# A product-key expert mixer: the dense gate array built by GpSimd's accumulating scatters instead of one-hot matmuls

## The reference, cut to what matters

```python
v1, i1 = lax.top_k(s1, PEER_TOPK)          # 16 of 128 rows
v2, i2 = lax.top_k(s2, PEER_TOPK)          # 16 of 128 columns
sc, pos = lax.top_k(comb, PEER_TOPK)       # 16 of their sums
experts = e1 * N_KEYS + e2
gate = jax.nn.softmax(sc, axis=-1)
ue = u[experts]
act = jax.nn.gelu(jnp.einsum('thkd,td->thk', ue, xt)) * gate
return jnp.einsum('thk,thkd->td', act, v[experts])
```

## Time and profile before

| | |
|---|---|
| median of 3 runs | 4715.58 us (4709.3 to 4719.58) |
| the profiled execution | 4713.71 us, of which its span is 4712.1 us |
| busy share of the span | PE 91%, PEld 78%, DVE 72%, ACT 37%, POOL 19% |
| mean granted clock of TensorE | 0.964 of full speed |
| moved by DMA | 913.53 MB, of 487554 packets 228722 under 512 B |
| stage of heads and bridge | 2004 to about 2545 us |
| gate stage | about 2545 to 3240 us |
| tail | about 3240 to 3624 us |
| mix and end | 3624 to 4712 us |

### The profile page before, as it was taken

The page is one execution under the profiler, slowest core; times in us unless marked ns, Lnnn a source line. Parts: engine busy times, 40 slices in busy tenths (PEclk is TensorE's granted clock), DMA queues, the critical chain, the costliest instruction groups (busy, mean ns, idle before and its releaser), DMA issues.

```text
span 4712.1 us, 67213 instructions
## 1 busy us (share of the span) xinstructions
PE 4302.6 (91%) x23716; PEld 3667.5 (78%) x23716; DVE 3409.5 (72%) x6418; ACT 1727.1 (37%) x3205; POOL 916.3 (19%) x885
## 2 busy tenths in 40 slices
PE   6999999999899799899999888888778999999998
PEld 3668877777788587798999777778778788888886
DVE  6530057777477543489997999997566998888888
ACT  3221146556566432322224555554111222222222
POOL 0000000000244210000001333333554222222221
PEclk9999999999999899999999999999899999999999
DMA  6642123332666553322223555556889999999996
GB/s 250 236 171 94 48 86 134 128 122 91 195 189 189 192 185 101 108 88 83 80 91 114 208 208 206 206 206 254 298 315 317 312 303 299 289 289 289 289 289 203
DMA packets 487554, 913.53 MB, mean 194 GB/s; under 512 B 228722, under 2 KB 277250, under 8 KB 482548
## 3 DMA queue, kind: packets, MB, share of 16 engines
q1 hardware_dynamic: 385684, 534.58, 34.7%
q0 software_dynamic: 95840, 363.13, 21.8%
q10 hardware_dynamic: 5760, 12.59, 0.7%
HBM read 722.20 MB, written 187.97 MB: 193 GB/s over the span
## 4 chain that ended last, share of the span: by engine, by line
PE 25%; DVE 24%; DMA 6%; issue 2%; POOL 1%; ACT 0%; SPq 0%; DVEq 0%; ACTq 0%
PE ph_gate_ps L2440 14%; PE ph_hid_ps L2440 7%; DVE held_tiles L2751 5%; DMA ph_ring<-in_u_rows,held_tiles 5%; DVE ph_row_hot L2744 5%; DVE ph_ring L2737 3%; DVE held_tiles L2747 2%; PE ph_hid_ps L2365 2%; PE ph_hid_ps L2355 2%; POOL ph_ring L2323 1%; DVE ph_hot L2627 1%; DVE ph_hot L2634 1%; DVE ph_u_lo L2572 1%; DVE ph_score L2599 1%; DVE ph_index L2601 1%
## 5 line engine op out<-in xcount | busy, mean ns | idle before, releaser
L2365 PE MATMUL ph_hid_ps<-ph_n_hi,ph_u_hi 128*128 128x384 f32 x2048 | 720.9, 352 | 89.6 <-DVE ph_u_lo L2572 89.6
L2365 PE MATMUL ph_hid_ps<-ph_n_lo,ph_u_hi 128*128 128x384 f32 x2048 | 709.0, 346 | 0.0
L2365 PE MATMUL ph_hid_ps<-ph_n_hi,ph_u_lo 128*128 128x384 f32 x2048 | 708.0, 346 | 0.0
L2365 PEld LDWEIGHTS ph_hid_ps<-ph_n_hi,ph_u_hi 128*128 128x128 f32 x2048 | 405.2, 198 | 99.4 <-DVE ph_u_lo L2572 99.2
L2323 POOL DMA_INDIRECT ph_ring<-in_u_rows,held_tiles x256 | 319.4, 1248 | 777.0 <-DVEq L2660 578.0
L2737 DVE CUSTOM_DVE_ANT_0 ph_ring<-ph_ring,ph_n_rows 128x1024 f32<-128x1024 f32 x256 | 308.0, 1221 | 148.2 <-DMA ph_ring<-in_u_rows,held_tiles 147.4
L2365 PEld LDWEIGHTS ph_hid_ps<-ph_n_lo,ph_u_hi 128*128 128x128 f32 x2048 | 404.7, 198 | 0.2
L2365 PEld LDWEIGHTS ph_hid_ps<-ph_n_hi,ph_u_lo 128*128 128x128 f32 x2048 | 403.0, 197 | 0.0
L2341 POOL DMA_INDIRECT ph_ring<-in_v_experts,ph_pick_again x256 | 242.6, 948 | 765.9 <-DVE held_tiles L2837 734.1
L2522 ACT ACTIVATE held_tiles<-held_tiles 128x128 bf16<-128x128 bf16 x768 | 246.1, 390 | 281.6 <-DVE held_tiles L2747 277.3
L2837 DVE SCALAR_TENSOR_TENSOR held_tiles<-ph_ring,ph_factor,held_tiles 128x1024 f32<-128x1024 f32 x254 | 324.5, 1278 | 0.0
(11 more groups left out here) (395 smaller groups left out, 10339.5 us busy)
## 6 DMA issues: line engine op xcount, KB each, us to landing
ph_u_raw<-in_tiles SPq DMA_DIRECT2D x136, 512.0 KB
ph_v_raw<-in_v_experts SPq DMA_DIRECT2D x124, 512.0 KB
scratch_hidden<-ph_hidden SPq DMA_DIRECT2D x128, 384.0 KB
scratch_gate_tiles<-ph_gates SPq DMA_DIRECT2D x12, 4096.0 KB
ph_u_raw<-scratch_hidden SPq DMA_DIRECT2D x124, 384.0 KB
ph_hidden<-scratch_gate_tiles SPq DMA_DIRECT2D x124, 384.0 KB
proj_w_ch<-in_w_ch SPq DMA_DIRECT2D x49, 512.0 KB, 3.8
mb_w_raw<-in_w_branch POOLq DMA_DIRECT2D x48, 512.0 KB, 3.9
```

The source lines that it names most:

```text
L2365: mm = pe.matmul(hid_halves[r][:, c, :], u[r][a][:, k, :], n2[b][:, k, c * CUT:(c + 1) * CUT], start=(k == 0 and a + b == 0), stop=(k == K ...
```

## The change

Gates are no longer computed on PE. A flat array of experts by tokens in memory (16384 x 768 floats, 50 MB) is cleared early in the kernel by 24 DMAs of 2 MB from ACT's queue, spread over the three turns of `project_token_major` (10, 10 and 4). For this the loop over turns is written out. When a head is done, POOL issues 96 indirect DMAs for it (6 token tiles x 16 picks). Each has 128 elements of 4 bytes, one per partition, and adds the weight to the array at expert * 768 + token. Before a head's DMAs, POOL waits until those of the head before it have landed. In heads 4 to 7 two gathers of u rows follow each three scatters. There is no gate stage: behind the bridge there are 80 tiles of the tail's kind, with 3 dot products each from the third on, the rest behind the last. `low` is always DVE's. The loads of the first four blocks of the mix wait for all scatters and for the last hidden stores. Gates are read from memory in rows of 3 KB, where they were pieces of 256 B.

```diff
-                with act.Fori(0, TURNS - 1) as i:
+                def clear(n):
+                    part = d["gates_flat"].rearrange("(c p n) a -> c p (n a)", c=ZEROS, p=P)
+                    act.dma_start(part[n], d["zeros"]).then_inc(zeroed, 16)
...
+                        if n < CLEARS[i]:
+                            clear(sum(CLEARS[:i]) + n)
+                CLEARS = (10, 10, 4)
+                for i in range(TURNS - 1):
...
                 turn(TURNS - 1, OUTS[1][2], True)
+                act.wait_ge(zeroed, 16 * ZEROS)
...
-TAIL_TILE0 = GATE_TILE0 + SM // 16
+TAIL_TILE0 = 1 + PH * PERIOD + BRIDGE
...
+    SCATTERS = MT * TOPK
...
-                    sync.dma_start(to[2][r].rearrange("p (b n) -> p b n", n=GATE_TOK), d["gate_tiles"][:, :, bass.ds(e, 1), :].rearrange(
-                        "b p a n -> p b (a n)")).then_inc(gate_in[r], 16)
+                    sync.dma_start(to[2][r], gate_rows[:, bass.ds(e, 1), :].rearrange("p a n -> p (a n)")).then_inc(gate_in[r], 16)
...
+                for h in range(PH):
+                    sync.wait_ge(scattered[h], 16 * SCATTERS)
+                for j in range(NJ):
+                    load_expert(j, j % 2, 1 if j >= 2 else None, staged_first)
...
-                pool.wait_ge(head_done, PH)
-                for n in range(NRING):
-                    gather_first(n)
-                for j in range(SM // PER_STEP):
...
-                    pool.tensor_tensor(u[r][1][:], u_raw[r][:], u[r][0][:].bitcast(F32), ALU.subtract).then_inc(u_lo[r], 1)
+                def scatter(h, n):
+                    t, k = divmod(n, TOPK)
+                    at = t * P + h * TOPK + k
+                    pool.indirect_dma_start(d["gates_flat"], bass.IndirectOffsetOnAxis(place_of[:, at:at + 1], 0), held[:, 2, at:at + 1], None,
+                                            compute_op=ALU.add).then_inc(scattered[h], 16)
...
+                for h in range(PH):
+                    pool.wait_ge(head_done, h + 1)
+                    if h >= 1:
+                        pool.wait_ge(scattered[h - 1], 16 * SCATTERS)
+                    if h == PH // 2:
+                        pool.wait_ge(hid_mm[1], PERIOD // 2 * (PH - 2) + 1)
+                    for n in range(SCATTERS):
+                        scatter(h, n)
+                        if h >= PH // 2 and n % 3 != 2:
+                            gather(next(gathers))
...
-                def step(j):
-                    tile(j % 2, (GATE_TILE0 + j) // 2)
-                    for b in range(NBANK):
...
-                                mm = pe.matmul(gate_ps[b][:, t, :], row_hot[b][:, t, :], term[n][b][:, t, :], start=(n == 0), stop=(n == 2))
...
-                    if y in FIRST_AT:
-                        high_parts(0, 0, FIRST_AT.index(y), staged_first)
                 act.wait_ge(dotted, PICKS)
                 act.activation(pick_dot, pick_dot, ACT.Gelu).then_inc(pick_gelu, 1)
+                for j in range(NJ):
+                    high_parts(0, 0, j, staged_first)
...
                 def experts_of(h, s, own):
-                    own.of(dve.tensor_copy(expert[:], placef[s][:]))
...
-                    own.of(dve.tensor_copy(chosen[:, 1, :, bass.ds(h, 1), :].rearrange("p t a k -> p t (a k)"), expert[:]))
+                    of, to = placef[s], place_of4[:, :, bass.ds(h, 1), :].rearrange("p t a k -> p t (a k)")
+                    own.of(dve.scalar_tensor_tensor(to[:, 0:MT, :], of[:, 0:MT, :], float(SM),
+                                                    token[:, 0:MT].unsqueeze(2).to_broadcast([P, MT, TOPK]), ALU.mult, ALU.add))
+                    own.of(dve.tensor_copy(to[:, MT:TT, :], of[:, MT:TT, :]))
...
-                    dots(3 if y in FIRST_AT else 5 + (y < 14) if y < TAIL - 1 else PICKS)
+                    dots(0 if y < 2 else 3 if y < TAIL - 1 else PICKS)
                 assert done == PICKS
+                for j in range(NJ):
+                    prepare(0, 0, j, staged_first)
```

More of the change, by code:

```diff
@@ L580, in project_token_major @@
         ahead_in = sp.sem("ahead_in")
+        zeroed = sp.sem("zeroed")
+        ZEROS = 24
+        d["gates_flat"] = nc.dram_tensor("scratch_gates_flat", (NK * NK * SM, 1), F32, kind="Internal").ap()
         OUTS = [("z", 2, ACT.Silu), ("v", 1, ACT.Copy)]
@@ L2053, in stage_peer_topk @@
         chosen = held[:, 0:3, :].rearrange("p a (t h k) -> p a t h k", t=TT, h=PH)
-        chosenT = held[:, 3:6, 0:SM]
+        place_of = held[:, 0, :].bitcast(U32)
+        place_of4 = place_of.rearrange("p (t h k) -> p t h k", t=TT, h=PH)
         pick_weight, pick_dot = held[:, 2, SM:S], held[:, 3, SM:S]
-        pick = held[:, 4, SM:S].bitcast(U32)
+        pick = place_of[:, SM:S]
+        token = sp.sb("token", [P, TT])
         keys = held[:, 6:8, :].rearrange("p a (h n) -> p (a h) n", n=2 * NK)
@@ L2084, in stage_peer_topk @@
             score_ps = first.enter_context(nc.psum_tensor("ph_score_ps", [P, TT, 2 * NK], F32))
[L2085 to L2094, removed]
+        bank = [sp.ps(f"bank{b}", [P, HALF]) for b in range(NBANK)]
         weight0, v0 = ([[sp.sb(f"{name}0{j}_{p}", [P, width], F32R)[:] for p in ("hi", "lo")] for j in range(NJ)]
@@ L2108, in stage_peer_topk @@
         staged = (v_raw, raw, gate)
-        staged_first = tuple([held[:, 2 * n + r, 0:SM if n else D] for r in range(2)] for n in range(3))
+        staged_first = ([held[:, r, :] for r in (6, 7)], [held[:, r, 0:SM] for r in (1, 3)], [held[:, r, 0:SM] for r in (4, 5)])
         acc = held
@@ L2119, in stage_peer_topk @@
         rstd = sp.sb("rstd", [P, TT])
-        out_ps = [gate_ps[b][:].rearrange("p t n -> p (t n)") for b in range(NBANK)] + [
+        out_ps = [bank[b][:] for b in range(NBANK)] + [
             hid_ps[n // 2][:, n % 2 * HALF:(n % 2 + 1) * HALF] for n in range(4)]
@@ L2125, in stage_peer_topk @@
         LAST_ORDER = (0, MT, 1, MT + 1) + tuple(range(2, MT))
[L2128 to L2132, removed]
         const_in = sp.sem("const_in")
@@ L2149, in stage_peer_topk @@
         head_done = sp.sem("head_done")
[L2150 to L2158, removed]
+        scattered = [sp.sem(f"scattered{h}") for h in range(PH)]
         raw_in = [sp.sem(f"raw_in{r}") for r in range(2)]
@@ L2204, in periods @@
             period(PH - 1, 1, False, True)
[L2206 to L2211, removed]
         with nc.Block() as block:
@@ L2319, in _, with gather @@
             def _(pool):
-                def gather_first(n):
+                def scatter(h, n):
[3 more added lines that the diff above has]
+                                            compute_op=ALU.add).then_inc(scattered[h], 16)
+                def gather(n):
                     if n >= NRING:
@@ L2324, in gather_first @@
                         pick[:, pick_at(n):pick_at(n) + 1], 0)).then_inc(u_row_in[n % NRING], 16)
[L2326 to L2336 removed]
+                gathers = iter(range(PICKS))
+                for h in range(PH):
[8 more added lines that the diff above has]
+                            gather(next(gathers))
                 pool.wait_ge(factor_step, 2)
@@ L2426, in turn @@
                             if first and b0 == 0 and b < NBANK:
[L2427 removed]
+                                pe.wait_ge(score_ready, PH + 1)
                             elif first and b0 == 0:
@@ L2716, in _ @@
                         experts_of(PH - 1, 1, own)
-                dve.wait_ge(turned, 6)
-                own = Steps(dve, share_step)
-                for n in range(2):
-                    own.of(dve.tensor_copy(share[n][:], chosenT[:, 2, :]))
-                    own.wait()
-                    own.of(dve.tensor_tensor(chosenT[:, 2, :], chosenT[:, 2, :], share[n][:], ALU.subtract))
-                    own.wait()
-                for b in range(NBANK):
-                    dve.sem_inc(gates_mm[b], 1)
                 done = 0
```

116 lines of the change are left out of this document (4 added, 112 removed).

## The result

The changed kernel takes 5159.35 us (median of 3 runs, 5154.29 to 5161.47), against 4715.58 us before: 1.0944 times as long, 95% interval 1.0927 to 1.0962. The prediction was 4737 us with a range up to 5080 us, so the sign was right and the size was not: 422 us are missing.

A forecast was written before the change was run, and what follows sets the result against it. POOL's ordered queue of 768 scatters and 256 gathers was to bound the kernel from 2103 to 3639 us. Span 4712 + 20.6 (into the mix) + 3 (clears) = 4736 us, 4737 us with 1.6 us around it; range 4570 to 5080 us.

The forecast's parts named there:

- Which engine bounds, and how the list is summed: From 2103 us to the mix: POOL's queue of scatters and gathers, with 0.30 us between DMAs, sets the pace till 3639 us.
- I take 0.99 us: POOL's price for one adding scatter: near a gather's 0.94 us, plus 0.05 us for 128 more reads; a pitch of 1.29 us.
- Rival A: Scatters on POOL cost more than 0.99 us, through the adding or slow memory engines; 4900 us at 1.2 us; chance 0.25.
- The waits inside DVE's operations: Indirect DMAs on POOL beginning inside two-array DVE operations wait for their end: 99 us in heads 0 to 3, 97 us later.
- Rival C: In the heads POOL runs free, as waits for DVE hold only where dot products follow one another: 4638 us; chance 0.08.
- The remark that a dearer scatter brings rather more of these waits: On POOL's path, 0.1 us more in a scatter was 77 us, and rather more with the waits behind DVE's operations.
- Landings between heads: POOL waits for one head's scatters to land before the next: 4 us each, 16 us in heads 0 to 3, 16 later.
- Into the mix: Between last scatter and mix: first four blocks loaded and prepared, first turn 22 us after the landing, +20.6 us on the span.
- The clears: In the projection, 50.3 MB cleared beside its own transfers: 0 to 10 us, 3 us in the sum.
- Rival D: The clears do not fit and hold the projection by 60 us: 4797 us; chance 0.05, with its own case for the scatter.
- PE's floor: In the 80 tiles behind the bridge PE alone needs 8.74 us each; with POOL out of the way, about 4385 us.
- rival B: Scatters on POOL are cheaper, or DVE's operations hold them less; 4590 us at 0.8 us, at the end about 4385; chance 0.22.

The follow-up runs named there:

- e3_clears: The kernel before with nothing added but the 24 clears of 2 MB and the written-out loop; 4714.08 us, 1.0003 times the kernel before.

## Why the prediction was wrong, point by point

- **Which engine bounds, and how the list is summed: right.** POOL without a pause from 2106 us, 0.30 us between DMAs, heads and mix nearly unchanged, PE standing behind the bridge (351 us at the longest where 150 were foretold, as the first gather comes at 2913.8 us and not at 2713) and then at POOL's pace.
- **"I take 0.99 us": the step that failed.** The gather was nearly right (0.99 us beside the scatters for 0.94, 13 us in all), and so was a write of 4-byte elements (0.98). The adding was sized by 128 more descriptors at plain DMAs' rate, 0.05 us; it costs 0.58 us. The term is 0.56 x 768 = 430 us, where 422 are missing. Plain DMAs showed what more pieces cost; no row showed a DMA that adds, and the step from one to the other had no ground. Rival A had it: at 1.5 us it gave 5130 us. It held 0.25, and the range's upper end, at 1.45 us, was 0.1 us too short, though the text itself had named a bound of 1.98 us and a slope of 77 us for each 0.1 us.
- **The waits inside DVE's operations: right in kind, 31 us too high.** 99 + 97 us were counted; 165 us are there in the changed kernel, and 906.0 - 768 x 0.98 = 153 and 280.5 - 256 x 0.98 = 29 in the run of writes. Rival C, no such waits in the heads, falls: 350 scatters up to 2845 us took 76 us above their own, nearly all of it in the 192 that begin before 2545 us. The remark that a dearer scatter brings rather more of these waits is wrong: they are 182 us with the cheap scatters and 165 with the dear ones.
- **Landings between heads: 14 us too high.** 32 us counted, 18 measured.
- **Into the mix: right.** 22 us counted from the last landing, 21.8 us measured; the mix behind it took 9 us more than the prediction let it.
- **The clears: right.** 3 us counted; the medians of e3_clears and of the kernel before beside it are 1.3 us apart, and the interval reaches from 3 us less to 6 us more. Rival D, 60 us, falls.
- **PE's floor: 43 us too high.** 8.3 us a tile, not 8.74. It enters the room of 396 us and rival B's end, not the sum.
- **The sum itself.** With writes, where the scatter costs the 0.98 us that was supposed, the kernel takes 4726.84 us against the 4737 of the prediction. In the changed kernel the small terms nearly cancel: gathers 14, waits for dot products 9, the mix 9 and others 3 us more than counted, the waits inside DVE's operations 31, the landings between heads 14 and the last landing 3 us less. With 0.566 x 768 = 435 us for the scatter's median of 1.556 us that leaves the 422 us.

## What to carry to other kernels

An ordered queue that 768 instructions pass through multiplies each error of their price by 768: where the trace has no row for the instruction, the range must go by the bounds of that price, and the nearest row stands for the same operation only, not for one that does something more with the data. Adding in a DMA was such a something here. And how much is moved to an idle engine decides: half of the gates on POOL, beside work of PE and DVE that stays, won 2.7%; all of them lost 9.4%.

## What the runs showed of the hardware

- An indirect DMA of 128 elements of 4 bytes costs POOL 1.55 us if it adds and 0.97 to 0.98 us if it writes (medians of 768); a gather of 128 rows of 4 KB costs 0.94 to 0.99 us. In the software queue a write is 32 packets and an adding scatter 144.
- An indirect DMA that begins inside a DVE operation on two arrays waits for its end (to some 0.1 us) and then takes its full price: a gather 0.94 us, an adding scatter 1.56 us, so that it shows 1.67 to 1.98 and 2.38 to 2.59 us behind operations of 1.2 us. In all 165 us in the changed kernel and 182 with writes.
- In one of six executions of one kernel all engines but POOL crept for four stretches of some 125 us, at one matmul in 2 to 3 us, with no wait in the trace; the other five were 340 us shorter (5068 and 4727 us).
